# Recurrent projections in the order decay, gates, keys, receptance, values, one a level

## The reference

```python
def token_mixer(u, ...):
    p = u @ w_in                       # pooling, hgrn, rwkv (8 tiles of 128), gla
    y_hgrn = rms_norm(gated_attention(q, 1 - f, v, log f)) * sigmoid(g)
    p_rw = p_rw + (prev - p_rw) * mu   # prev: the token before
    rr, rk, rv, xw, xa, xg = split(p_rw, [256, 512, 768, 832, 896])
    sigma = sigmoid(w0 + tanh(xw) @ w2); a = sigmoid(a0 + xa @ a2); g = sigmoid(xg) @ g2
    kk = unit(rk * k_k);  k = rk * (1 + (a - 1) * k_a);  w = exp(-e^-0.5 * sigma)
    # S = S diag(w) - (S kk)(kk a)^T + v k^T ;  o = S r ; bonus = sum(r * k * r_k)
    y_gla = rms_norm(gated_attention(q, k, v, log a)) * silu(g)
    return concat(y_pool, y_hgrn, y_rwkv, y_gla) @ w_out
```

## Time and profile before

| | |
|---|---|
| median of 3 runs | 1809.31 us (1805.96 to 1809.87) |
| the profiled execution | 1808.35 us, span 1806.5 us |
| mean granted clock of TensorE | 0.965 |
| TensorE busy (matmul) | 1727.6 us, 96% |
| VectorE, ScalarE, GpSimd busy | 873.5, 675.2, 131.2 us |

### The profile page before, as it was taken

One profiled execution on the slowest core, in us unless ns is written; L12 is line 12 of the kernel. 1 busy time (PEld: TensorE's weight loads), 2 busy tenths in 40 slices (PEclk: granted clock), 3 DMA queues, 4 the chain that ended last, 5 costly groups with the idle time before them and its releaser, 6 DMA issues.

```text
span 1806.5 us, 22170 instructions
## 1 busy us (share of the span) xinstructions
PE 1727.6 (96%) x8706; PEld 1406.7 (78%) x8706; DVE 873.5 (48%) x1171; ACT 675.2 (37%) x1016; POOL 131.2 (7%) x127
## 2 busy tenths in 40 slices
PE   7999999999999899999999989979998899999997
PEld 5777778778778688888887778769986678888885
DVE  5633444633436465444335775764345554444322
ACT  5145664225564333333223543443121433232221
POOL 0001002001001000000004000001320100000000
PEclk9999999999999999999999999956999899999998
DMA  5322213322212132223333211200001223233331
GB/s 178 135 69 71 82 59 99 124 81 73 81 59 82 58 117 94 94 94 96 97 99 129 71 59 49 66 9 1 1 21 44 82 82 100 99 100 93 96 96 47
DMA packets 41177, 143.91 MB, mean 80 GB/s; under 512 B 4865, under 2 KB 4881, under 8 KB 40817
## 3 DMA queue, kind: packets, MB, share of 16 engines
q1 hardware_dynamic: 37152, 130.61, 22.4%
q0 software_dynamic: 2192, 8.73, 1.5%
q10 hardware_dynamic: 1728, 3.15, 0.5%
HBM read 140.37 MB, written 2.10 MB: 79 GB/s over the span
## 4 chain that ended last, share of the span: by engine, by line
PE 80%; DVE 12%; ACT 5%; issue 2%; DMA 0%; DVEq 0%; POOLq 0%; POOL 0%; ACTq 0%; SPq 0%
PE bank L447 22%; PE bank L448 21%; PE bank L449 21%; PE bank L429 9%; DVE sb_E L1092 2%; DVE sb_w_low L1092 2%; PE bank L435 2%; DVE sb_near L1471 1%; PE bank L646 1%; PE bank L625 1%; PE bank L582 1%; ACT sb_E L1799 1%; ACT sb_w_high L1799 1%; DVE sb_xg_low L1100 1%; DVE sb_x L1100 1%
## 5 line engine op out<-in xcount | busy, mean ns | idle before, releaser
L1092 DVE TENSOR_TENSOR sb_w_low<-sb_raw,sb_w_high 128x1024 fp32r<-128x1024 f32 (+1 forms) x253 | 310.3, 1227 | 394.1 <-ACT sb_w_high L1799 387.6
L447 PE MATMUL bank<-sb_xg_high,sb_w_high 128*128 128x512 f32 x1176 | 470.9, 400 | 29.3 <-DVE sb_xg_low L1100 18.2
L449 PE MATMUL bank<-sb_xg_high,sb_w_low 128*128 128x512 f32 x1176 | 462.0, 393 | 0.0
L448 PE MATMUL bank<-sb_xg_low,sb_w_high 128*128 128x512 f32 x1176 | 461.8, 393 | 0.0
L1799 ACT ACTIVATE sb_w_high<-sb_raw 128x1024 fp32r<-128x1024 f32 (+1 forms) x253 | 263.2, 1040 | 355.7 <-PE bank L449 330.9
L447 PEld LDWEIGHTS bank<-sb_xg_high,sb_w_high 128*128 128x128 f32 x1176 | 223.0, 190 | 97.0 <-issue 35.8
L449 PEld LDWEIGHTS bank<-sb_xg_high,sb_w_low 128*128 128x128 f32 x1176 | 223.0, 190 | 47.9
L448 PEld LDWEIGHTS bank<-sb_xg_low,sb_w_high 128*128 128x128 f32 x1176 | 223.3, 190 | 45.5 <-issue 1.2
L447 PE MATMUL bank<-sb_h_high,sb_w_high 128*128 128x512 f32 x352 | 136.9, 389 | 0.0
L448 PE MATMUL bank<-sb_h_low,sb_w_high 128*128 128x512 f32 x352 | 136.9, 389 | 0.0
L449 PE MATMUL bank<-sb_h_high,sb_w_low 128*128 128x512 f32 x352 | 136.9, 389 | 0.0
(11 more groups left out here) (332 smaller groups left out, 2130.4 us busy)
## 6 DMA issues: line engine op xcount, KB each, us to landing
sb_raw<-w_ffn_in SPq DMA_DIRECT2D x88, 512.0 KB, 3.3
sb_raw<-w_ffn_out SPq DMA_DIRECT2D x32, 512.0 KB, 3.5
sb_raw<-w_tok SPq DMA_DIRECT2D x24, 512.0 KB, 3.7
sb_raw<-w_mix_f SPq DMA_DIRECT2D x18, 512.0 KB, 3.2
sb_raw<-w_rot SPq DMA_DIRECT2D x16, 512.0 KB, 3.7
sb_raw<-w_qk SPq DMA_DIRECT2D x16, 512.0 KB, 3.3
sb_raw<-w_out SPq DMA_DIRECT2D x16, 512.0 KB, 3.3
sb_raw<-w_ffn_out SPq DMA_DIRECT2D x16, 384.0 KB, 3.1
```

Of the source, the lines that this page charges most:

```text
L447: e.matmul(out, w[0], v[0], start=first, stop=False)
L448: e.matmul(out, w[0], v[1], start=False, stop=False)
L449: return e.matmul(out, w[1], v[0], start=False, stop=last)
L1092: e.tensor_tensor(out, a, b, op).then_inc(*v.up(*signal))
```

## The change

The projections run in the order 6, 7, 2, 3, 0, 1, 4, 5, one in each of fills 0 to 7. The operand steps become single functions, called at set levels:

| fill | TensorE | VectorE | ScalarE |
|---|---|---|---|
| 1 | | | tanh, after the projection |
| 2 | decay and gate in, before the projection | | sigma, a gate, sigmoid |
| 3 | gate out, before | sums of sigma | gate out landed |
| 4 | | | key squares (into tiles 4, 5 of `mixed`), gla's gate |
| 5 | key norm, before | key floored, before | exponentials of the decay |
| 6, 7 | projections 4, 5 | | "own" of 4, 5 waits for key norm |
| 8 | key turned | keys: kk, kkE, bI | key spread |
| 9 | | receptance: k, bonus operand, kI, rE | |
| after | bonus sums | | bonus |

The a gate, sigma and cum move out of `xg`'s room; `tmp` goes. At the ends of the layers and of the mixers VectorE writes `xg_low` one tile later than it adds, and ScalarE converts the next weight ahead of the last square.

```diff
+RWKV_ORDER = (6, 7, 2, 3, 0, 1, 4, 5)
...
+        m.a_gate = r.room("a_gate", 2, SEQ)
+        m.ga = region(gate_at, end).room("ga", SEQ)
...
-        m.sigma, m.cum, m.a_gate, m.tmp = (r.room(n, 2, SEQ) for n in ("sigma", "cum", "a_gate", "tmp"))
+        m.sigma, m.cum = region(rwkv_at, end).room("sigma", 2, SEQ), self.square
...
         def fill_gla(n):
             if n < 2:
                 next(values_g)
+            if n == 2:
+                decay_and_gate_in()
+            if n == 3:
+                gate_out()
+            if n == 5:
+                key_norm()
+            if n < 8:
                 next(projections)
-            elif n < 6:
-                next(projections)
-                if n in (2, 4):
-                    next(projections)
-                if n == 5:
-                    p.mark("xg read", MIX_NORM)
-            else:
-                next(operand_prep)
+            if n == 7:
+                p.mark("xg read", MIX_NORM)
+            if n == 8:
+                key_turned()
...
     def added(n, f, factor):
         v.wait_ge(*of("out", n, f))
         stt(x[:, f, :], bank("out", n, f)[:, :], factor, x[:, f, :], ALU.mult, ALU.add, "out added", n, f)
-        if NEXT_NORM[n] != LAST_NORM:
-            xg_low(NEXT_NORM[n], f)
-        if NEXT_NORM[n] == MID_NORM and f >= 2:
-            weigh_square(f - 2)
...
                     added(n, f, 1.0)
+
+                    if f:
+                        xg_low(NEXT_NORM[n], f - 1)
+                    if NEXT_NORM[n] == MID_NORM and f >= 2:
+                        weigh_square(f - 2)
+        xg_low(NEXT_NORM[n], KT - 1)
         use()
...
+        def keys():
+            v.wait_ge(*of("xg read", MIX_NORM))
             for f in range(2):
                 v.wait_ge(*of("key turned", f))
...
-            tt(m.kkE, kk, m.tmp, ALU.mult, *STEP)
+            tt(m.kkE, kk, before, ALU.mult, *STEP)
...
             tt(x[:, f, :], x[:, f, :], bank("mix last", f)[:, :], ALU.add, "out added", MIX_NORM, f)
-            xg_low(NEXT_NORM[MIX_NORM], f)
+            if f:
+                xg_low(NEXT_NORM[MIX_NORM], f - 1)
+        xg_low(NEXT_NORM[MIX_NORM], KT - 1)
...
-                    added(n, f)
-        use()
+                    xg_high(NEXT_NORM[n], f)
+                    if f == KT - 1:
+                        use()
+                    square(NEXT_NORM[n], f)
...
+                if f in (4, 5):
+                    a.wait_ge(*of("key norm"))
...
+        def key_squares():
+            a.wait_ge(*of("rwkv mixed", 3))
+            for f in range(2):
+                act(m.mixed[:, 4 + f, :], m.mixed[:, 2 + f, :], "key squares", func=ACT.Square,
+                    scale=mem.col("rwkv_k_k", f))
...
+        def key_spread():
+            a.wait_ge(*of("xg read", MIX_NORM))
+            a.wait_ge(*of("key inverse"))
+            act(heads(flat(m.kI)), small[:, 176:192].unsqueeze(2).to_broadcast([P, 16, 64]), "key spread")
```

More of the change, by code:

```diff
@@ L163, in unit_order @@
     order += [t["w_mix_ga"]] + mixer_tiles(14, 16, 15, 17)
-    values, projections = mixer_group(1), mixer_tiles(*range(2, 10))
+    values, projections = mixer_group(1), mixer_tiles(*(2 + f for f in RWKV_ORDER))
     order += values[0:3] + [projections[0], values[3]] + projections[1:]
@@ L844, in operand_steps, with gate_out @@
                     group(banks[i][:, :], [(m.lora[r, 0, blk(f)], m.mixed[r, 6, :])], what + " in", f)
[L845 to L851, removed]
+        def gate_out():
             for half in range(2):
@@ L857, in operand_steps, with key_norm, key_turned @@
                           "gate out", half)
+        def key_norm():
+            i = take(("key norm",), ("key floored",))
+            p.wait_ge(*of("key squares"))
+            for t in range(TT):
+                for f in range(2):
+                    at = 4 * t + 2 * f
+                    group(banks[i][:, at:at + 2], [(m.mixed[:, 4 + f, blk(t)], mem.table("same_head")[:, 0:P:64])],
+                          "key norm")
+        def key_turned():
             for f in range(2):
@@ L871, in operand_steps @@
                           "bonus in")
-            yield
-        projections, operand_prep = rwkv_steps(), operand_steps()
+        projections = rwkv_steps()
         def fill_gla(n):
@@ L1581, in rwkv_steps, with decay_sums, key_floor @@
                 yield
-        rr, rk, kk, eI = m.mixed[:, 0:2, :], m.mixed[:, 2:4, :], m.bI, m.rE
-        def operand_steps():
-            yield
+        rr, rk, kk = m.mixed[:, 0:2, :], m.mixed[:, 2:4, :], m.bI
+        before, eI = m.sigma, m.cum
+        def decay_sums():
+            v.wait_ge(*of("sigma", 1))
+            for f in range(2):
+                scan(m.cum[:, f, :], m.sigma[:, f, :], "sigma summed", f)
+            tt(before, m.cum, m.sigma, ALU.subtract, "sigma before")
+        def key_floor():
             norms = small[:, 176:192]
@@ L1622, in fill_gla @@
                 next(values_g)
-                if n == 0:
-                    finish_hgrn()
-                next(projections)
[L1626 to L1631, removed]
+            if n == 0:
+                finish_hgrn()
+            if n == 5:
+                key_floor()
+            if n < 8:
+                next(projections)
+            if n == 3:
+                decay_sums()
+            if n == 8:
+                keys()
+            if n == 9:
+                receptance()
         finish_gla = linear_attention("gla", fill_gla)
-        for _ in operand_prep:
-            pass
         inverse(m, finish_gla)
@@ L2161, in rwkv_steps @@
         def rwkv_steps():
-            for f in range(8):
+            for k, f in enumerate(RWKV_ORDER):
                 use()
@@ L2179, in operand_steps, with gate_out @@
                     act(out[:, f, :], bank(what, f)[:, :], what, f, func=ACT.Sigmoid, bias=mem.col(bias, f))
+            a.wait_ge(*of("rwkv mixed", 7))
             act(m.mixed[:, 7, :], m.mixed[:, 7, :], "rwkv sigmoid", func=ACT.Sigmoid)
[L2181 to L2184, removed]
+        def gate_out():
             for half in range(2):
@@ L2223, in mixers @@
         finish_gla = linear_attention("gla", fill_gla)
-        for _ in operand_prep:
-            pass
+        a.wait_ge(*of("bonus in"))
+        act(small[:, 112:128], bank("bonus")[:, 0:16], "bonus")
         preset("X", m.X, "factors read")
```

90 lines of the change are left out of this document (40 added, 50 removed).

## The result

The changed kernel takes 1822.32 us (median of 4 runs, 1819.94 to 1822.97); the kernel before, beside it, 1809.59. The ratio is 1.0075, 95% interval 1.0059 to 1.0091: slower by 13 us. I had forecast 1808.5, no change, in a range of 1794 to 1816. So the forecast is wrong, and the time lies outside its range too.

A forecast was written before the change was run, and what follows sets the result against it. TensorE, with 80% of the chain, was taken as the bound, through its holes and half clock. Terms -8.7 (layer 1's end), -6.8 (mixers' end) and +15.2 (gla) gave -0.3 us, about 1808.5 us, range 1794 to 1816.

The forecast's parts named there:

- Part 2: Gated attention (gla): operands awaited ahead of projections in TensorE's queue open holes and drop the clock; value products +15.2 us.
- Holes forecast 4.0, 4.6, 6.5, 10.7: TensorE's idle us in gla, ahead of the products needing tanh, the last sigmoid, key squares and key spread.
- Values forecast at 1222.9: Start of gla's value products, against 1207.7 before: 15.2 us later, with half clock behind the holes.
- half-way: Rival in gla: early holes cost no clock, values start only 5 to 7 us later; whole 1799 us; chance 0.20.
- the clock stays full from the values on: Rival in gla: value products and what follows run at full clock, 20 us less; whole 1788 us; chance 0.12.
- Part 1: Ends of layer 1 and of the mixers: VectorE's later xg low removes waits and half clock; -8.7 and -6.8 us.
- first term: End of layer 1: VectorE needs some 2.7 us a tile, against 3.49, and so keeps step with TensorE.
- Forecast -8.7: End of layer 1: 5.6 us of TensorE's waits and 3.4 us of lost clock go, less rounding.
- The signs named for the end of layer 1: No wait of TensorE over 1 us there, and a full clock.
- Forecast -6.8: Mixers' end: tiles at 1.45 to 1.6 us against 2.33; gain 7.6 us, or 5.9 with another clock fall.
- under 2.5 was the sign: Mixers' end: TensorE's waits would total under 2.5 us.
- The collision: Rival at both boundaries: GpSimd's square sums slow VectorE's xg low, 1.07 us each; +7, whole 1816 us; chance 0.13.

The follow-up runs named there:

- e5: Changed kernel with decay and gate in, gate out and key norm issued behind their level's projection on TensorE, VectorE's key floor moved likewise; 1807.91 us, ratio 0.9999.
- e10: The changed kernel unaltered, traced once more; hgrn stage 159.4 us, gla to values 96.1 us, stage to the mixers' root 211.5 us.
- e1: Kernel before with only the edits at the layer and mixer ends (xg_low one tile later, weight converted ahead of the last square); 1805.14 us, ratio 0.9984.
- e9: The kernel before unaltered, traced once more; hgrn stage 159.2 us against 157.1 in its first trace, stage to the mixers' root 210.3 us.
- e3: e1 with GpSimd's sums of squares left out at the end of layer 1 and of the mixers, only signals given; 1794.10 us, ratio 0.9924.
- e6: e5 with the turned keys behind the last two levels' scores and VectorE's near-done mark set behind level 64; 1800.67 us, ratio 0.9956.
- e4: e1 with the two norms' sums of squares made by VectorE instead of GpSimd; 1804.26 us, ratio 0.9972.

## Why the prediction was wrong

**Part 2 was right in mechanism and size.** Holes forecast 4.0, 4.6, 6.5, 10.7; idle times measured 4.06, 4.75, 6.47, 10.69. Values forecast at 1222.9, measured 1222.92. That the two agree to the hundredth is luck: gla begins 0.4 us earlier than in before, and the stage grew by 15.7 us where the forecast has 15.2. The falls of the clock behind each hole came too, and with them the rival "half-way" fell; "the clock stays full from the values on" fell by the 0.52 and 0.50 measured there. The one trace row that I had for it, a fall behind a single level's scores, was the right one to go by. e5 shows that TensorE's queue order does most of it. The Trainium skill ("TensorE: Matmul & The Clock Gate", section "HAM oscillation — how this bites in real kernels") has short bursts with waits between them pay the cold clock each time; e5 and after agree (1.99 against 3.78 us for the same 8 matmuls).

**Part 1 failed at its first term**, "A tile then costs it 0.69 + 1.04 + 0.75 and 0.1 between each: some 2.7 us, against 3.49". Measured: 0.69 + 1.73 + 0.75 and 0.1 between each, 3.49. The step that failed is the price of xg low, taken over as 1.04 (and 0.75 at the mixers) into a loop in which it now runs beside GpSimd's sum. Forecast -8.7, measured -3.0. That does not come from a shorter period: the last four adds start 1.5 us earlier but the loop behind them is no faster, and the last split ends 2.2 us earlier, now that its weight is converted ahead of the last square (at 590.15, before at 594.99). The signs named for the end of layer 1 failed with it: two waits over 1 us (1.3 for xg low, 1.4 for the split) and 3.4 us of half clock. Forecast -6.8 at the mixers' end, with a tile in 1.45 to 1.6 us; measured are adds 1.65, 2.52 and 1.69 apart, and nothing that stands out of the scatter of that stage (211.5 to 213.0 in after, e10 and e1, 210.3 to 213.7 in before and e9). TensorE's waits there went from 4.9 to 3.3 us in the first pair, where under 2.5 was the sign. e3 gives the first forecast back in full and the second in part once GpSimd's sums are gone.

How I misread it: I took 1.04 for a partial overlap, a mild case, and 1.82 for the rare one. They are one and the same event. Before, one tile later than in the earlier trace rows, VectorE, ScalarE and GpSimd:
```profile
588.81 1.04 DVE L1100 SCALAR_TENSOR_TENSOR sb_xg_low<-sb_x,sb_mid_gain,sb_xg_high 128x512 fp32r<-128x512 f32 x1 [0.79 <-ACT sb_xg_high L1799]
589.95 0.75 DVE L1100 SCALAR_TENSOR_TENSOR sb_cos<-sb_square,sb_mid_weight,sb_cos 128x512 f32<-128x512 f32 x1
...
587.29 0.63 ACT L1799 ACTIVATE sb_square<-sb_x 128x512 f32<-128x512 f32 x1 [2.01 <-DVE sb_cos L1100]
...
588.00 1.30 POOL L2356 TENSOR_TENSOR sb_square_sum<-sb_square_sum,sb_square 128x512 f32<-128x512 f32 x1 [2.20 <-ACT sb_square L1799]
```
The sum ended at 589.30, and xg low, started at 588.81, ended 0.55 behind it. It was short only because it started late, and it started late because of the very stall that the change takes out. Without the stall xg low starts 0.12 behind the sum and is held for the whole of it. The loop is in lockstep: VectorE's weighing of a square frees ScalarE's next square, whose end starts the sum just as VectorE comes to xg low, and the end of xg low lets VectorE weigh the next square. That ring is closed in both kernels and it alone gives the period: weighing 0.75, square 0.63, sum 1.29, 0.55 to the end of xg low, and some 0.09 at each of the three changes of instruction, 3.49 in all. The stall of 0.79 was not part of it, so taking it out could gain nothing there; what was cut from the stall came back in the hold.

**The rivals.** The collision stood among them with 0.13 and a price of 1.07 us a tile, against a gain that I had left at -5 and -3.5. The event was right and its price too small: the real remainders were -3.0 and about 0. It counted four tiles at each boundary; at the mixers' end six xg lows are held, by 3.6 us together, where before none was. With the two remainders my sum is -3.0 + 0 + 15.2 = +12, against 13 measured. The Trainium skill ("SBUF — State Buffer", section "Who interferes with whom") says that a VectorE instruction with two SBUF inputs contends with a GpSimd instruction that reads SBUF, and that such contention is an exclusive lock. I set it aside for the 1.04 rows; it was right, and those rows agree with it once one looks at ends instead of durations.

Small slips in the working change nothing above: 27.5 less 17 is a hole of 10.5 and not 10.7, the parts of the chances add up to 0.33 for the same and 0.24 for slower, and 0.69 + 1.04 + 0.75 with three times 0.1 is 2.8 and not 2.7.

## What to carry to other kernels

When a duration of an instruction varies, compare its end with the end of what ran on the other engines before calling it a mild case; an end that keeps a fixed distance is a lock, and its price is set by when the instruction starts. Before removing a stall, ask what the next instruction will then run beside. A product that waits for another engine belongs behind the independent work of its level in an in-order queue, and the fall of the clock behind a hole can cost as much again: from the changed kernel to e5, gla and its values lost 5.4 us of idle time (27.8 to 22.4) and 12.5 us in all.

## What the runs showed of the hardware

- 14 xg lows of the changed kernel began while a square sum of GpSimd ran: 12 ended 0.55 us behind the end of that sum; the other two began in the sum's last 0.01 us and took 0.75, as alone. 17 weight splits did so too and ended 0.82 us behind (the 12 of 128x768, 0.96 alone) or 1.08 behind (the 5 of 128x1024, 1.23 alone). All five adds with an operand in a PSUM bank that began under a sum took 0.69 us, as alone. The hold works the other way as well: three sums that began 0.3 to 0.5 us before the end of an xg low or a split took 1.47, 1.56 and 1.60 instead of 1.29.
- TensorE can stay at half clock for 27 us without a hole (e6, 1219 to 1246), in a stretch of small products, where the value products shortly before, small as well, ran at 0.95. What decides between the two I did not settle.
- One program gave stages that differ by 2 to 3 us from one execution to the next (hgrn 157.1 and 159.2 in before), and the longer one has more half clock (17.1 against 10.2 us). That is not the whole of it: e3 and e4 have 10.2 as well and take 158.5 and 158.4. A difference of that size in a single pair of traces is not a finding.
